# A hybrid encoder on one core: the start of the SBUF work area moves from 32 modulo 128 bytes to 0 modulo 128

## The reference

```
layer 0 mixer:  proj = x @ w_in (1024 x 1792)
                8-head grouped attention, RMS-normalised q/k, axial rotary, softmax
                conv module: GLU, depthwise conv of 31 taps, LayerNorm, swish
                concat(attention, conv) @ w_out (1024 x 1024)
layer 1 mixer:  proj = x @ w_in (1024 x 6144)
                4-head retention, forward and backward scans with decays, summed
                per-head norm, silu(g) * y, @ w_out (2048 x 1024)
each layer:     x = LN(4 ** 0.25 * x + mixer(x))
                x = LN(4 ** 0.25 * x + (silu(x @ w_gate) * (x @ w_up)) @ w_down)
```

## Time and profile before

| | |
|---|---|
| median of three runs | 1456.62 us (1451.8 to 1459.44) |
| profiled execution, span from the first to the last instruction | 1449.7 us |
| TensorE matmuls | 7068, busy 97% of the span |
| VectorE, ScalarE, GpSimd busy | 46%, 31%, 15% |
| mean granted TensorE clock | 0.986 of full |

### The profile page before, as it was taken

How to read it: one execution, slowest core, us unless ns; L and a number is a source line. 1 busy time by engine, 2 the same in 40 slices (tenths; PEclk the granted TensorE clock), 3 DMA queues, 4 the chain that set the end, 5 groups by cost and what they waited for, 6 DMA issues and landing times.

```text
span 1449.7 us, 17321 instructions
## 1 busy us (share of the span) xinstructions
PE 1405.9 (97%) x7068; PEld 1189.9 (82%) x7068; DVE 668.9 (46%) x829; ACT 456.2 (31%) x546; POOL 218.0 (15%) x188
## 2 busy tenths in 40 slices
PE   8878899999999999999999999999999999999997
PEld 8767787888888888889898988888888888888886
DVE  3899972733333322165546264554363333332225
ACT  3456553332232221133223242423142322322211
POOL 3686731300000000033201002000030000000000
PEclk9989979999999999999999999999999999999999
DMA  5210010223323332304222122222222233223221
GB/s 183 87 59 0 30 59 30 88 87 104 99 87 102 111 106 90 112 31 136 71 80 78 58 87 87 87 88 87 88 87 88 87 96 107 87 94 137 87 87 59
DMA packets 84017, 124.18 MB, mean 86 GB/s; under 512 B 2688, under 2 KB 61312, under 8 KB 83968
## 3 DMA queue, kind: packets, MB, share of 16 engines
q1 hardware_dynamic: 83968, 123.49, 25.6%
HBM read 121.39 MB, written 2.10 MB: 85 GB/s over the span
## 4 chain that ended last, share of the span: by engine, by line
PE 88%; DVE 6%; POOL 2%; ACT 2%; issue 1%; DMA 1%; SPq 0%; DVEq 0%; POOLq 0%; ACTq 0%
PE ps L1238 22%; PE ps L1240 22%; PE ps L1239 22%; PE ps L1314 19%; DVE acc L919 2%; POOL w_lo L376 1%; PE ps L1446 1%; PE ps L1251 1%; ACT w_hi L372 1%; PE ps L1420 1%; DVE row_max L1002 1%; DMA x_tok<-in_x 1%; DVE w_lo L376 1%; PE ps L1526 0%; DVE probT_lo L1019 0%
## 5 line engine op out<-in xcount | busy, mean ns | idle before, releaser
L376 DVE TENSOR_TENSOR w_lo<-raw,w_hi 128x2048 fp32r<-128x2048 f32 x101 | 232.0, 2297 | 504.7 <-ACT w_hi L372 504.7
L1238 PE MATMUL ps<-xT_hi,w_hi 128*128 128x512 f32 (+1 forms) x1120 | 389.8, 348 | 0.5 <-POOL w_lo L376 0.3
L1239 PE MATMUL ps<-xT_lo,w_hi 128*128 128x512 f32 (+1 forms) x1120 | 388.6, 347 | 0.0
L1240 PE MATMUL ps<-xT_hi,w_lo 128*128 128x512 f32 (+1 forms) x1120 | 388.4, 347 | 0.0
L372 ACT ACTIVATE w_hi<-raw 128x2048 fp32r<-128x2048 f32 x109 | 208.3, 1911 | 443.5 <-PE ps L1240 262.5
L1238 PEld LDWEIGHTS ps<-xT_hi,w_hi 128*128 128x128 f32 x1120 | 212.3, 190 | 27.4 <-POOL w_lo L376 1.1
L1239 PEld LDWEIGHTS ps<-xT_lo,w_hi 128*128 128x128 f32 x1120 | 212.3, 190 | 26.6
L1240 PEld LDWEIGHTS ps<-xT_hi,w_lo 128*128 128x128 f32 x1120 | 212.3, 190 | 26.3
L574 POOL TENSOR_SCALAR var_eps<-var_eps 128x1 f32<-128x1 f32 x16 | 6.2, 388 | 857.2 <-ACT squares L773 857.2
L1238 PE MATMUL ps<-w_hi,xT_hi 128*128 128x512 f32 (+1 forms) x320 | 121.7, 380 | 0.0
L1239 PE MATMUL ps<-w_lo,xT_hi 128*128 128x512 f32 (+1 forms) x320 | 121.5, 380 | 0.0
(11 more groups left out here) (167 smaller groups left out, 1771.5 us busy)
## 6 DMA issues: line engine op xcount, KB each, us to landing
raw<-in_l_w_in SPq DMA_DIRECT2D x31, 1024.0 KB, 5.1
raw<-in_l_ffn_w_gate SPq DMA_DIRECT2D x22, 1024.0 KB, 5.2
raw<-in_l_ffn_w_up SPq DMA_DIRECT2D x22, 1024.0 KB, 5.2
raw<-in_l_ffn_w_down SPq DMA_DIRECT2D x22, 1024.0 KB, 4.7
raw<-in_l_w_out SPq DMA_DIRECT2D x12, 1024.0 KB, 4.9
x_tok<-in_x SPq DMA_DIRECT2D x4, 512.0 KB, 6.1
out<-x_tok SPq DMA_DIRECT2D x8, 256.0 KB, 2.1
ln_gb<-in_l_ln_mix_g SPq DMA_DIRECT2D x2, 512.0 KB, 5.2
```

The source lines that it names most:

```text
L376: eng.tensor_tensor(w_lo[ch.s][:], raw[ch.s][:], f32(w_hi[ch.s][:]), ALU.subtract)\
L1238: nc.tensor.matmul(dst, a[0], b[0], start=start, stop=False)
L1239: nc.tensor.matmul(dst, a[0], b[1], start=False, stop=False)
L1240: return nc.tensor.matmul(dst, a[1], b[0], start=False, stop=stop)
```

## The change

The top of the placed area is rounded up to a multiple of 128 (`P` is 128) before `work` is taken from it. With 4000 bytes of small tensors, `work` moves up by 96 bytes, to 4096 bytes behind the first of them. All tensors placed relative to `work` move with it, and no instruction is added, taken away or reordered.

```diff
         row_sum = place("row_sum", [P, STEPS], F32)
         row_inv = place("row_inv", [P, STEPS], F32)
 
+        top[0] = -(-top[0] // P) * P
         work = top[0]
         hT_hi = place("hT_hi", [P, NH, SEQ], F32R, work)
         hT_lo = place("hT_lo", [P, NH, SEQ], F32R, work + NH * SEQ * 4)
```

## The result

The changed kernel took 1447.8 us (median of six runs, 1443.99 to 1449.24), the kernel before 1456.68 us (six runs, 1451.57 to 1459.44). The ratio of their times is 0.9943, with a 95% interval of 0.9926 to 0.996. The forecast was 1447.6 us.

The account below looks back on a forecast made before the run. TensorE was taken to bound the kernel, busy 1405.9 of 1449.7 us. Terms 3.3 + 3.1 + 0.9 + 0.2 + 1.4 = 8.9, say 9.0 us, took 1456.6 to 1447.6 us; range 1442 to 1456.

Parts of the forecast that it names:

- The pace and its cause: 512-column matmuls: operands 32 apart modulo 128 take 233.3 ns, at the same place 226.7; aligning them gains 6.67 ns each.
- the region: Rival, chance 0.15: pace goes by whether operands lie inside the work area, not by address; nothing changes, 1456.6 us.
- the order of `part()`: Rival, chance 0.08: the helper `part()` has its own 233.3 ns; only `yT` gains, 1.6 us, to 1455.0 us.
- 32 apart modulo 128: Pairs of `w` with `hT`, `catT`, `yT`: this distance was said to hold them at 233.3 ns instead of 226.7.
- I count no gain for the first nine matmuls behind a break: Matmul rows after breaks: pace takes time to settle, so nine matmuls are left out of each long row's gain.
- Down projections 3.3 and 3.1 us: FFN down projections of layers 0 and 1: 495 and 459 matmuls gaining 6.67 ns each.
- Output projection of layer 0, 0.9: Layer 0's output projection: 135 of 144 matmuls gain, 0.9 us; its other 48, in short groups, not counted.
- Output projection of layer 1, 1.6: Layer 1's output projection: 0.2 us from twelve blocks of twelve plus 1.4 us from one long row.
- Lies 6.9 us above that span: Median of runs, 1456.62 us, against the profiled span of 1449.7; the difference was carried over to the forecast.
- The slower rival (taps): Convolution on VectorE: new distance of `zpad` and `acc` lengthens taps, 0.84 us each, up to 1469 us; chance 0.04.
- Attention, put at 0: Attention stretch: moved tensors of other engines could give at most 2.3 us; none counted, -1 to +2 us in the range.
- Two ports for the two operands: Skill page's objection: TensorE's independent SBUF read ports make relative place irrelevant, so the sum would be 0 instead of 9.0.

Follow-up runs that it names:

- everything at 32: Changed kernel with the whole allocation and the work area starting at 32 modulo 128, so operands keep the same place; 1442.29 us, ratio 0.9924 to the kernel before.

## Why the prediction was right, and where it was not

- **The pace and its cause.** Right: 233.3 to 226.7 ns in `hT`, `catT` and `yT`, nothing in the long rows of the pairs that kept their distance, and the same in reverse when the weights were moved instead. Four kinds of pairs at one pace and three at the other in the trace before were enough to name what matters, the place of the two operands relative to each other; the experiments were needed to exclude the region and the order of `part()`. What inside the chip makes such reads slower, no run shows.
- **The modulus.** The step "32 apart modulo 128" failed as it was put. The runs show 256: at 128 apart the pace is 232.4 ns. The rounding to 128 worked because 4000 bytes leave 160 modulo 256, and so reach the next multiple of 256 when they reach the next of 128. That was luck: with 128 bytes less of small tensors the same line would have left the pairs 128 apart, and six sevenths of the loss with them. The prediction did note that the pairs become 0 apart "even modulo 512", but drew nothing from it.
- **The starts.** The step "I count no gain for the first nine matmuls behind a break" rested on the scores, and was misread: there is no break ahead of them, and their slow start was itself an effect of place, gone in the changed kernel. The 504 of the down projection, which follow without a break too, run at 226.7 ns from the first.
- **The terms of the sum.** Down projections 3.3 and 3.1 us: measured 117.60 - 114.24 = 3.36 and 109.21 - 106.09 = 3.12 us, and the 60 matmuls behind the second piece brought the end no nearer, as said. Output projection of layer 0, 0.9: measured 33.60 - 32.66 = 0.94, and 0.12 in two groups of twelve that were not counted. Output projection of layer 1, 1.6: measured 1.96. Its long row gave 1.4 as said, but the blocks of twelve 0.5 in place of 0.2, since many settle sooner than after nine. Not counted at all were 0.4 us of starts of scores and token tiles in retention, and 0.09 behind the first down projection. In all 10.0 us against 8.9.
- **Span and median.** "Lies 6.9 us above that span" was wrong as a measure of what lies around a span: the changed kernel's profiled run took 1447.29 us with a span of 1445.5, so 1.8 us lie around it. The profiled execution of before was one with the fuller clock (0.986), and 5 of the 6.9 us were that. Since the gain was taken from the median, the forecast did not suffer. That 1447.6 came within 0.2 us of the median is luck: the sum was 1 us too small, and the medians differ by 8.9 and not by 10.0, since they mix clocks: two of the six runs before took 1451.6 and 1451.8 us, as runs at the fuller clock do, and none of the six after has more than 0.983.
- **Other engines.** Right that nothing there pays or costs: 600 and 692 ns stay. The slower rival (taps) did not come: 1287 to 1300 ns on the mean, 0.7 us over 53 taps. Attention, put at 0 with up to 2 us in the range, gave nothing (experiment with everything at 32).
- **The pages of the Trainium skill.** Two ports for the two operands, in "TensorE: Matmul & The Clock Gate" (What happens when you issue a matmul), would make the relative place indifferent; the runs contradict that reading, for the place of one operand relative to the other costs 6.7 ns, 16 cycles of 2.4 GHz, in 512 columns. The 16-byte lines of "SBUF — State Buffer" (Specifications) don't predict it either: 32, 64 and 128 bytes are all whole lines and all cost.

## What to carry to other kernels

When two stages of equal matmuls, both without idle time and at the same granted clock, differ in the distance between starts, list the addresses of their moving and stationary operands; here that was the whole difference. For fp32r products of 512 columns, put both at the same place modulo 256, and products that follow each other too; it need not be 0, and rounding to 128 is only half a guard. Compare runs at like granted clock, or from a point behind the stretch in which the clock varies, or a gain of 0.7% can hide behind 0.35% of clock.

## What was not expected of the hardware

A pair that is 32 bytes apart makes 512-column matmuls slower (227 to 233 ns) but 256-column matmuls quicker (119.9 to 118.3 ns). Why the sign turns is not known; no other width was tried, and it doesn't turn for every distance: with a moving `w` 4 bytes off, the 256-column token tiles average 123.1 ns, 120.0 in the changed kernel. A third of the pairs apart costs two thirds of the full loss (231.1 ns between 226.7 and 233.3). And 132 bytes with `w` stationary cost almost nothing (226.9 ns), where 4, 32 and 96 cost 5.7 to 7.6.
